# Evicting a chunk between the two halves of a weight split in a hybrid decoder trunk

## The reference

```python
for layer in range(2):
    shift, scale, gate = split(silu(c) @ ada_w[layer, 0] + ada_b[layer, 0], 3)
    hn = rmsnorm(x, norm_g[layer, 0]) * (1 + scale) + shift
    y = rglru_mlstm_mixer(hn, ...) if layer == 0 else stick_breaking_mixer(hn, w_qkv, w_out)
    x = x + gate * y
    shift, scale, gate = split(silu(c) @ ada_w[layer, 1] + ada_b[layer, 1], 3)
    hn = rmsnorm(x, norm_g[layer, 1]) * (1 + scale) + shift
    x = x + gate * (silu(hn @ w1) * (hn @ w3)) @ w2        # hidden width 5632
return rmsnorm(x, final_g)
```

## Time and profile before

| | us |
|---|---|
| median of 3 executions | 2385.03 (2383.54 to 2386.46) |
| the profiled execution | 2383.7 |
| its span | 2381.6 |
| PE busy (share of the span) | 2305.2 (97%) |
| DVE busy | 1774.5 (75%) |
| ACT busy | 951.8 (40%) |
| POOL busy | 192.9 (8%) |
| mean busy share of the DMA engines, q1 | 68.3% |
| mean granted TensorE clock | 0.989 of full |

### The profile page before, as it was taken

The page is one execution under the profiler, slowest core; times in us unless marked ns, Lnnn a source line. Parts: engine busy times, 40 slices in busy tenths (PEclk is TensorE's granted clock), DMA queues, the critical chain, the costliest instruction groups (busy, mean ns, idle before and its releaser), DMA issues.

```text
span 2381.6 us, 35557 instructions
## 1 busy us (share of the span) xinstructions
PE 2305.2 (97%) x12570; PEld 1971.4 (83%) x12570; DVE 1774.5 (75%) x2216; ACT 951.8 (40%) x1101; POOL 192.9 (8%) x177
## 2 busy tenths in 40 slices
PE   5999999999999999999999999998999999999998
PEld 3668888888888888888878888787888888888887
DVE  6766789888788887788986656598887566656677
ACT  2011344544334443343455545434443344433443
POOL 0000005100000000000611101151000000000014
PEclk9999999999999999999999999999999999999999
DMA  9998778577777777777766666475776555555554
GB/s 379 422 405 360 290 293 318 192 292 283 281 272 292 281 275 271 290 277 290 270 241 238 250 234 242 180 296 227 285 282 226 180 191 193 191 182 192 192 196 159
DMA packets 86616, 619.79 MB, mean 260 GB/s; under 512 B 10264, under 2 KB 10520, under 8 KB 11544
## 3 DMA queue, kind: packets, MB, share of 16 engines
q1 hardware_dynamic: 85680, 617.79, 68.3%
q10 hardware_dynamic: 872, 1.15, 0.1%
HBM read 616.80 MB, written 2.10 MB: 260 GB/s over the span
## 4 chain that ended last, share of the span: by engine, by line
PE 90%; DMA 4%; DVE 4%; issue 1%; ACT 1%; SPq 0%; POOL 0%; DVEq 0%; POOLq 0%; ACTq 0%
PE ps L1117 48%; PE ps L1115 12%; PE ps L1120 12%; PE ps L1067 7%; DMA adaw<-ada_dram 4%; PE ps L1054 3%; PE ps L1031 1%; DVE adaw L676 1%; DVE wlow L668 1%; PE ps L1033 1%; PE ps L1078 1%; ACT whigh L490 0%; PE ps L1084 0%; PE ps L1262 0%; PE ps L1162 0%
## 5 line engine op out<-in xcount | busy, mean ns | idle before, releaser
L490 ACT ACTIVATE whigh<-raw 128x1024 fp32r<-128x1024 f32 x704 | 744.8, 1061 | 1087.2 <-PE ps L1117 1050.7
L668 DVE TENSOR_TENSOR wlow<-raw,whigh 128x1024 fp32r<-128x1024 f32 x704 | 874.7, 1260 | 363.9 <-ACT whigh L490 356.0
L1117 PE MATMUL ps<-hn,whigh 128*128 128x512 f32 x3232 | 1018.2, 396 | 0.4 <-DVE wlow L668 0.4
L1117 PE MATMUL ps<-mid,whigh 128*128 128x512 f32 x1856 | 586.3, 396 | 3.6 <-DVE wlow L668 3.6
L1117 PEld LDWEIGHTS ps<-hn,whigh 128*128 128x128 f32 x3232 | 493.2, 189 | 0.9 <-issue 0.7
L1115 PE MATMUL ps<-hn,wlow 128*128 128x256 f32 x1616 | 449.9, 278 | 0.0
L1120 PE MATMUL ps<-hn,wlow 128*128 128x256 f32 x1616 | 448.2, 277 | 0.0
L676 DVE CUSTOM_DVE_ANT_0 adaw<-adaw,cact 128x2048 f32<-128x2048 f32 x152 | 350.6, 2308 | 28.0 <-DMA adaw<-ada_dram 28.0
L1115 PEld LDWEIGHTS ps<-hn,wlow 128*128 128x128 f32 x1616 | 303.3, 188 | 73.9
L1120 PEld LDWEIGHTS ps<-hn,wlow 128*128 128x128 f32 x1616 | 303.9, 188 | 69.2
L1117 PEld LDWEIGHTS ps<-mid,whigh 128*128 128x128 f32 x1856 | 284.3, 189 | 5.1 <-DVE wlow L668 4.9
(11 more groups left out here) (213 smaller groups left out, 1484.4 us busy)
## 6 DMA issues: line engine op xcount, KB each, us to landing
raw<-wts_dram SPq DMA_DIRECT2D x386, 1024.0 KB, 4.8
adaw<-ada_dram SPq DMA_DIRECT2D x152, 1024.0 KB, 6.7
adaw_more<-ada_dram SPq DMA_DIRECT2D x24, 1024.0 KB, 10.0
raw<-ada_dram SPq DMA_DIRECT2D x16, 1024.0 KB, 12.5
work<-wts_dram SPq DMA_DIRECT2D x6, 1024.0 KB, 11.1
x<-xT_dram SPq DMA_DIRECT2D x4, 512.0 KB, 11.3
out_dram<-x SPq DMA_DIRECT2D x4, 512.0 KB, 2.7
cact<-c_row_dram SPq DMA_DIRECT2D x1, 1024.0 KB, 5.0
```

The source lines that it names most:

```text
L490: act.activation(whigh[:, (2 * s + h) % 4, :], raw[:, s, h * HALF:(h + 1) * HALF], ACT.Copy)\
L668: dve.tensor_tensor(wlow[:, half, :], raw[:, s, h * HALF:(h + 1) * HALF], whigh[:, half, :].bitcast(F32), ALU.subtract).then_inc(S["low_re ...
L1117: ins = pe.matmul(ps[:, s, :], whigh[:, half, w], src[:, kk, :, :], start=kk == 0, stop=kk == kts - 1, skip_group_check=True)
```

## The change

In every slot of the bodies named above, the second half of the split moves behind the eviction, on DVE and on ACT; on DVE in `up` behind the whole product too. In slot 3 of `out` and `down` the first half now comes ahead of the update. The units of a slot come last. The second halves that a short chunk uses are 512 columns (tiles 8 to 11) instead of 1024: 28 splits on each engine. The last two short bodies of the first FFN are written out instead of a loop of two, so that the width of each split is known; PE, SP and POOL keep their order.

```diff
-            bodies(b + UP[2] + 2, DOWN - 2, down + "short", q=2, i0=2)
+            body(b + UP[2] + 2, down + "short", 2, 2, 0, 0)
+            body(b + UP[2] + 3, down + "short", 2, 3, 0, 0)
...
+def second_width(kind, s, i):
+
+    if "short" in kind and (s < 2 or not isinstance(i, int) or i < DOWN - 1):
+        return (GROUPS[2] - HK) * P
+    return HALF
...
         @block.scalar
                 for s in range(CH):
-                    if splits_ahead(n, s, kind, units):
-                        split(*split_lead(n, s))
+                    ahead = splits_ahead(n, s, kind, units)
+                    if ahead:
+                        split(*split_lead(n, s), 0)
                     if kind in STORED:
...
                         act.activation(work[:, 2 + s // 2, :], work[:, s // 2, :], ACT.Silu).then_inc(S["silu_ready"], 1)
+                    if ahead:
+                        split(*split_lead(n, s), 1, second_width(kind, s, i))
                     for stage in inner.get(s, ()):
                         between(*stage)
...
         @block.vector
-            def split(n, s):
-
-                for h in range(2):
-                    dve.wait_ge(S["high_ready"], n * 8 + 2 * s + h + 1)
-                    half = (2 * s + h) % 4
-                    dve.tensor_tensor(wlow[:, half, :], raw[:, s, h * HALF:(h + 1) * HALF], whigh[:, half, :].bitcast(F32),
-                                      ALU.subtract).then_inc(S["low_ready"], 1)
+            def split(n, s, h, width=HALF):
+
+                dve.wait_ge(S["high_ready"], n * 8 + 2 * s + h + 1)
+                half = (2 * s + h) % 4
+                dve.tensor_tensor(wlow[:, half, 0:width], raw[:, s, h * HALF:h * HALF + width],
+                                  whigh[:, half, 0:width].bitcast(F32), ALU.subtract).then_inc(S["low_ready"], 1)
...
-                    update_first = s == CH - 1 and kind[:3] in ("out", "dow")
-                    if not update_first and splits_ahead(n, s, kind, units):
-                        split(*split_lead(n, s))
+                    ahead = splits_ahead(n, s, kind, units)
+                    if ahead:
+                        split(*split_lead(n, s), 0)
...
                             sum_halves(work[:, 4 + j, :], s)
-                            units_of(pair, units, s)
                             dve.wait_ge(S["silu_ready"], count + 1)
...
                         update_x(n, s, kind.replace("short", ""), q, i)
-                        if update_first and units >= 0:
-                            split(*split_lead(n, s))
-                    if kind[:2] != "up":
-                        units_of(pair, units, s)
+                    if ahead:
+                        split(*split_lead(n, s), 1, second_width(kind, s, i))
+                    units_of(pair, units, s)
                     for stage in inner.get(s, ()):
                         between(*stage)
```

More of the change, by code:

```diff
@@ L480, in _ @@
         def _(act):
-            def split(n, s):
-                act.wait_ge(weight_loaded[s], weight_count(n, s))
-                for h in range(2):
-                    if isinstance(n, int) and n == OUT0 and s < 2:
-                        act.wait_ge(S["unit_done"], EARLY + FULL_RINGED + 2)
-                    else:
-                        act.wait_ge(S["halves_multiplied"], n * 8 + 2 * s + h + 1)
-                    act.activation(whigh[:, (2 * s + h) % 4, :], raw[:, s, h * HALF:(h + 1) * HALF], ACT.Copy)\
-                       .then_inc(S["high_ready"], 1)
+            def split(n, s, h, width=HALF):
+                if h == 0:
+                    act.wait_ge(weight_loaded[s], weight_count(n, s))
+                if isinstance(n, int) and n == OUT0 and s < 2:
+                    act.wait_ge(S["unit_done"], EARLY + FULL_RINGED + 2)
+                else:
+                    act.wait_ge(S["halves_multiplied"], n * 8 + 2 * s + h + 1)
+                act.activation(whigh[:, (2 * s + h) % 4, 0:width], raw[:, s, h * HALF:h * HALF + width], ACT.Copy)\
+                   .then_inc(S["high_ready"], 1)
             def full_body(n, kind, i):
@@ L498, in full_body @@
                     if splits_ahead(n, s, kind, 0):
-                        split(*split_lead(n, s))
+                        for h in range(2):
+                            split(*split_lead(n, s), h)
                     for stage in FULL_ACT_FIRST.get(slot, ()):
```

## The result

The change takes 2366.23 us (median of 4, 2365.25 to 2367.6) against 2384.68 us (median of 4) for the kernel before on the same chip: the ratio is 0.9923, 95% interval 0.991 to 0.9937. That is 18.45 us less, where 20.7 were forecast; 2366.23 lies inside the range, 1.9 us above the predicted time. The profiled execution took 2365.77 us with a span of 2363.9.

What follows compares the result with a forecast made beforehand. PE is busy 97% of the span, so only its idle and slow time can be won. Terms 5.8 + 4.5 + 4.5 + 6.6 + 1.25 - 1.3 - 0.6 = 20.7 us, from 2385.0 to 2364.3 us; range 2360.5 to 2371.5.

Steps and rivals of the forecast that it cites:

- Terms 1, 2 and 4: PE waits gone: first down-stage chunks 5.8 us, first FFN's short stage 4.5 us, `k` body to `vs` body 6.6 us.
- Term 2: First chunk of first FFN's short down stage: wait and half-clock stretch behind it go, 4.5 us; 2.9 if clock still falls.
- Term 3: Short stage with units, where DVE is behind: narrower splits nearly remove four PE waits, 4.5 us gained, at least 2.
- Term 5: Third norm: first half made before PE ends, so 1.25 us less PE idle time ahead of the reciprocal's L1154.
- Term 6: Last `vs` body: two copies before the last half start the second output projection 1.27 us later, a loss of 1.3 us.
- Term 7: Clock behind the norms: slow stretch after PE's restart may be longer or shorter, -0.6 us, between +1 and -3.
- (a): Rival: POOL's squares hold DVE more in the new order, short stage loses 2.1 us instead of gaining 4.5; 2371, chance 0.08.
- (b): Rival: gains refilled by later DVE waits or clock, four new slow stretches at 1.7 us each; 2382.8, chance 0.05.
- (c): Rival: unit's tile load, issued later behind the weight's, comes late and stalls DVE, costing 35 us; 2400, chance 0.03.

Runs made afterwards that it cites:

- The three parts alone: Kernel before with one edit each: unit last in `up`, 2377.35 us; `q`/`k` eviction between split halves, 2377.29 us; short chunks' second halves 512 columns, 2381.08 us.

## Why the prediction was right, and where its steps were off

**What bounds the kernel** was read rightly: only PE's waits and their echo in the clock could be won, and pricing each from like row to like row (idle time and about 0.26 us more) gave Terms 1, 2 and 4 within 0.1 us each. The three parts alone give 7.2 + 7.2 + 3.4 = 17.8 us, near the whole 18.45, but that is no proof that they do not touch each other: 1.6 of the first 7.2 us are the clock's at another place, the width is worth 3.4 alone and 5.0 beside the new order, and the second half behind the eviction in `up`, `out` and `down` has no run of its own.

**Term 2**: "Without the gap I take it that the fall goes too" held, in the change and with the unit's move alone.

**Term 3** was mis-sized, 3.1 us for 4.5. The bounds of DVE's body were right: from unit to unit it takes 17.5 us twice (from 1123.31 and from 1132.34) and then 17.9 (1140.81 to 1158.68), inside "17.1 to 17.9". The step that failed is the lead, "Its first halves are done about 3 us before PE wants them at the start of the stage", and with it the 0.2 us taken as left. The first half of every second chunk stands behind a unit. DVE's first such half in the stage, and the one at which PE waits first:

```profile
1126.21 1.23 DVE L678 TENSOR_TENSOR wlow<-raw,whigh 128x1024 fp32r<-128x1024 f32 x1 [0.31 <-issue]
...
1144.09 1.23 DVE L678 TENSOR_TENSOR wlow<-raw,whigh 128x1024 fp32r<-128x1024 f32 x1
```

```profile
1145.37 0.50 PE L1125 MATMUL ps<-mid,whigh 128*128 128x512 f32 x1 [0.24 <-DVE wlow L678]
```

The first is done at 1127.43, and PE starts the chunk that uses it, the third, at 1128.24: a lead of 0.8 us. At the fifth chunk the lead is 0.3 (1136.31 and 1136.59), and at the seventh, ninth and eleventh PE waits 0.24, 0.28 and 0.34 us. The prediction's own figures for full chunks held the answer: a first half is done 6.9 us after PE's end, and in the short stage it is wanted after 2 x 4.17 = 8.3, which leaves 1.4 us, not 3.

**Term 5** gave 1.0 for 1.25: with one half (1.22 us) instead of two (2.77) ahead of the unit 1.55 us were won, but beside POOL the unit takes 2.70 us where it took 2.28, and the update starts 0.1 us later behind PE's last matmul.

**Term 6** had the wait right (the row is 3.97 us, "about 4.1" forecast) and left the clock to the range; it came. DVE and PE there (timeline):

```profile
1500.62 1.27 DVE L765 COPY work<-ps 128x512 f32<-128x512 f32 x2
1501.82 1.21 DVE L678 TENSOR_TENSOR wlow<-raw,whigh 128x1024 fp32r<-128x1024 f32 x1
```

```profile
1503.13 0.77 PE L1039 MATMUL ps<-mid,whigh 128*128 128x512 f32 x1 [3.97 <-issue]
```

The copies stand where the last half was, and PE starts 0.1 us behind that half. The half clock then lasts 6.8 us from 1501.85 where before it lasted 3.4 from 1518.7: 5.5 us of it fall on work instead of 3.4, which costs about 1.0.

**Term 7** came out at its value by luck, through two parts of which the forecast named one: behind the third norm PE starts (1612.16) 5.7 us before the slow stretch ends, where before it was 3.5, which costs 1.1; a small wait on `wlow` behind that norm (0.41 us idle, 0.5 with its price) is gone.

**The step that failed outright** is the sentence "In the other norms the last slot has no unit and ends in time". At the second norm the last slot is short: PE needs 1.39 us from its half to its end, and DVE's first half, begun when ACT has made its own, runs past that. PE at the second norm, before and after, then DVE after:

```profile
1200.31 0.61 PE L1148 MATMUL ps<-ones,work 128*128 128x1 f32 x4 [1.00 <-POOL work L454]
1202.23 1.01 PE L1148 MATMUL ps<-ones,work 128*128 128x1 f32 x4 [1.31 <-POOL work L448]
```

```profile
1188.79 0.61 PE L1156 MATMUL ps<-ones,work 128*128 128x1 f32 x4 [0.23 <-POOL work L462]
1192.39 1.01 PE L1156 MATMUL ps<-ones,work 128*128 128x1 f32 x4 [2.99 <-POOL work L456]
```

```profile
1188.36 1.46 DVE L678 TENSOR_TENSOR wlow<-raw,whigh 128x1024 fp32r<-128x1024 f32 x1 [0.90 <-ACT whigh L497]
1189.74 0.47 DVE L716 SCALAR_TENSOR_TENSOR work<-ps,mod,x 128x256 f32<-128x256 f32 x1
```

PE's last matmul starts at 1188.17 and is over by 1188.6; the update starts at 1189.74. From that last matmul to the spreading of rstd it is 5.78 us (to 1193.95), before it was 4.89 (1198.91 to 1203.80). With the update first again the 0.9 us are back (4.66 us).

**The rivals.** (a) did not happen: POOL does hold DVE, but the new order adds nothing to it, as the full halves show. (b) did not happen: no wait came back in the long stages, and half clock was added at two places that had it already (1.0 and 1.1 us), not at four new ones. (c), the tile that comes late, did not happen in the change, and the forecast weighed it by the right rows; but its sentence "wanted some 11 us after" rests on the second half standing ahead of the unit, which the prediction did not name as the condition. With the unit ahead of it the mechanism is there at once, through SP's queue, and costs 80 us.

## What to carry to other kernels

When work is moved within an in-order engine, look at which semaphore it releases and what is queued behind the waiter on the DMA issuing engine: a load queued behind another load's wait can close a loop that is longer than the compute, and then an order that looks equal on the engine itself costs 80 us of 2366, 3%. Price a short PE wait from like row to like row rather than by its idle time, and look at short chunks apart: a piece that fits ahead of PE's end in a full chunk does not fit in one of 12 tiles. And when a part run alone gains more than its theory says, look in its trace for places that the edit does not touch.

## What the runs showed of the hardware

The half clock behind a gap does not follow from the gap alone. At the second output projection, the same place of the program, eight of the kernels wait 3.97 or 3.98 us: six of them, the change and its repeat among them, have 1.2 GHz for 6.8 us, and two, with full halves and with the update first, for 3.4. The other six, the kernel before among them, wait 2.87 us: five have 1.2 GHz for 3.4 us, and the one with only the unit moved has none. Each is one profiled execution. The windows of the change and of the kernel with the update first (us, busy of PE, PEld, DVE, ACT, POOL, granted clock, DMA share, GB/s):

```profile
1501.85:1505.25 3.40, 2.12 (x7) 1.86 (x8) 3.39 (x4) 0.00 (x0) 0.00 (x0) 0.50 0.79 289
1505.25:1508.65 3.40, 3.40 (x12) 2.92 (x12) 0.16 (x1) 0.00 (x0) 0.00 (x0) 0.50 1.00 424
```

```profile
1501.90:1505.30 3.40, 2.80 (x9) 2.44 (x10) 2.87 (x4) 0.00 (x0) 0.00 (x0) 0.51 0.76 280
1505.30:1508.70 3.40, 3.40 (x21) 2.98 (x21) 0.00 (x0) 0.00 (x0) 0.00 (x0) 0.99 1.01 426
```

The slow stretch starts at nearly the same moment of the run in both (1501.85 and 1501.9 us), while PE restarts at 1503.13 in the one and at 1502.50 in the other, so PE's busy time in the first 3.4 us is 2.12 against 2.80 us. Of the eight kernels with 3.97 us, the six with the long stretch restart PE 0.9 to 1.8 us after the clock has fallen, the other two 0.6 us after it and 1.0 us ahead of it. So an edit elsewhere that shifts this moment by some tenths of a microsecond can move the time by 1 us and more, either way, and differences of that size between two of these kernels are not the edit's unless the trace shows them at its place. What decides it beyond these rows was not tried.
